# Expert weights in long rows per partition, the hidden rows turned on VectorE, six weight buffers

## What is computed

```python
def expert_choice_ffn(h, w_router, w_gate, w_up, w_down):
    b, s, d = h.shape                       # 1, 256, 1024
    cap = CAPACITY_FACTOR * s // N_EXPERTS  # 32 tokens for each of 16 experts
    aff = jax.nn.softmax((h @ w_router).astype(jnp.float32), axis=-1)
    gates, idx = lax.top_k(jnp.swapaxes(aff, 1, 2), cap)
    xs = jax.vmap(lambda hb, ib: hb[ib])(h, idx)
    hid = jax.nn.silu(jnp.einsum('becd,edf->becf', xs, w_gate)) * jnp.einsum('becd,edf->becf', xs, w_up)
    out = jnp.einsum('becf,efd->becd', hid, w_down) * gates[..., None].astype(h.dtype)
    return jax.vmap(lambda ob, ib: jnp.zeros((s, d), h.dtype).at[ib.reshape(-1)].add(ob.reshape(-1, d)))(out, idx)
```

## Time and profile before

| | |
|---|---|
| median of three runs | 2667.03 us (2659.16 to 2667.18) |
| the profiled execution's own time | 2660.17 us |
| its span, first to last instruction | 2658.4 us |
| TensorE matmul, busy | 2062.7 us, 78% of the span |
| VectorE, busy | 723.2 us, 27% |
| ScalarE, busy | 538.4 us, 20% |
| moved from HBM | 736.88 MB, mean 278 GB/s |

### The profile page before, as it was taken

The page is one execution under the profiler, slowest core; times in us unless marked ns, Lnnn a source line. Parts: engine busy times, 40 slices in busy tenths (PEclk is TensorE's granted clock), DMA queues, the critical chain, the costliest instruction groups (busy, mean ns, idle before and its releaser), DMA issues.

```text
span 2658.4 us, 30415 instructions
## 1 busy us (share of the span) xinstructions
PE 2062.7 (78%) x13332; PEld 1230.3 (46%) x13332; DVE 723.2 (27%) x1115; ACT 538.4 (20%) x816; POOL 105.8 (4%) x145
## 2 busy tenths in 40 slices
PE   8899899989998998896666766666676667666765
PEld 8779798887897886774111111111111112111211
DVE  4554544454545445543000000000000000000001
ACT  5444333343444333332000000000000000000000
POOL 2100100011001001100000000000000000000000
PEclk9879899997998999878665666666666756565566
DMA  8225376742434766327999999999999999999997
GB/s 263 80 88 167 104 237 211 226 136 81 143 128 148 224 221 207 124 110 282 391 381 390 410 381 370 393 392 377 371 408 383 372 366 412 382 367 375 409 385 240
DMA packets 269380, 739.92 MB, mean 278 GB/s; under 512 B 10768, under 2 KB 137232, under 8 KB 236352
## 3 DMA queue, kind: packets, MB, share of 16 engines
q1 hardware_dynamic: 266896, 731.29, 75.9%
q0 software_dynamic: 2352, 6.69, 0.7%
HBM read 736.88 MB, written 1.05 MB: 278 GB/s over the span
## 4 chain that ended last, share of the span: by engine, by line
DMA 47%; PE 40%; DVE 7%; ACT 3%; issue 2%; SPq 1%; POOL 0%; DVEq 0%; ACTq 0%
PE PS L310 39%; DMA WB<-in_w_up 13%; DMA WB<-in_w_gate 12%; DMA WB<-in_w_down 6%; DMA J<-in_w_gate 2%; DMA J<-in_w_up 2%; DMA N<-in_w_up 2%; DMA N<-in_w_gate 2%; DVE WL L1380 2%; ACT WH L917 1%; DMA C<-in_w_gate 1%; DMA C<-in_w_up 1%; SPq L2215 1%; DMA N<-in_w_down 1%; DMA J<-in_w_down 1%
## 5 line engine op out<-in xcount | busy, mean ns | idle before, releaser
L310 PE MATMUL PS<-WB,XS 128*32 128x352 f32 x2880 | 379.5, 672 | 130.3 <-DMA WB<-in_w_up 74.8
L1380 DVE TENSOR_TENSOR WL<-W,WH 128x2048 fp32r<-128x2048 f32 x136 | 313.7, 2307 | 244.0 <-ACT WH L917 244.0
L310 PE MATMUL PS<-WB,S 128*32 128x512 f32 (+1 forms) x1072 | 207.2, 885 | 143.1 <-DMA WB<-in_w_down 141.3
L310 PE MATMUL PS<-HTh,WH 128*128 128x256 f32 x1064 | 307.7, 289 | 5.7 <-DVE HTl L1831 2.6
L917 ACT ACTIVATE WH<-W 128x2048 fp32r<-128x2048 f32 x141 | 269.0, 1908 | 178.7 <-PE PS L310 174.7
L310 PE MATMUL PS<-HTl,WH 128*128 128x256 f32 x1064 | 301.5, 283 | 0.0
L310 PE MATMUL PS<-HTh,WL 128*128 128x256 f32 x1064 | 301.4, 283 | 0.0
L310 PEld LDWEIGHTS PS<-WB,XS 128*32 128x32 f32 x2880 | 98.7, 140 | 403.7 <-DMA WB<-in_w_up 176.3
L1375 DVE SCALAR_TENSOR_TENSOR S<-S,PS 128x352 f32<-128x352 f32 (+1 forms) x110 | 63.3, 588 | 758.5 <-ACT S L1341 719.7
L310 PEld LDWEIGHTS PS<-HTh,WH 128*128 128x128 f32 x1064 | 204.4, 192 | 9.3 <-DVE WL L1380 3.3
L310 PEld LDWEIGHTS PS<-HTl,WH 128*128 128x128 f32 x1064 | 204.6, 192 | 0.3
(11 more groups left out here) (282 smaller groups left out, 2430.4 us busy)
## 6 DMA issues: line engine op xcount, KB each, us to landing
WB<-in_w_gate SPq DMA_DIRECT2D x91, 1408.0 KB, 28.3
WB<-in_w_up SPq DMA_DIRECT2D x89, 1408.0 KB, 30.0
WB<-in_w_down SPq DMA_DIRECT2D x112, 1024.0 KB, 15.9
W<-in_w_in SPq DMA_DIRECT2D x31, 1024.0 KB, 5.6
W<-in_w_ada SPq DMA_DIRECT2D x24, 1024.0 KB, 5.3
W<-in_w_gate SPq DMA_DIRECT2D x22, 1024.0 KB, 7.8
W<-in_w_up SPq DMA_DIRECT2D x22, 1024.0 KB, 5.6
W<-in_w_down SPq DMA_DIRECT2D x22, 1024.0 KB, 5.1
```

What stands on the lines that cost most here:

```text
L310: return e.matmul(o, l, r, start=start, stop=stop, skip_group_check=True)
L1380: e.tensor_tensor(M.WL[i][:, :], M.W[:, 2048 * (m % NW):2048 * (m % NW) + 2048], M.WH[i][:, :].bitcast(F32), ALU.subtract).then_inc(*up("l ...
```

## The change

All 48 expert matrices are read in the same way. A matrix is seen as 128 long rows: partition p gets rows 8p to 8p+7 of w_gate or w_up, or rows 22p to 22p+21 of w_down, 90,112 contiguous bytes in either case. Four chunks cut these in pieces of 22,528 bytes, each one transfer over 128 partitions. There are six buffers of that size, five in a new `WB` and one over constants and work space in `C1`. A buffer now serves two k of gate or up (freed after the second), or 11 half rows of 512 columns of w_down.

As a contraction chunk k of gate and up now holds the rows 8p+k, everything that makes the other operand steps by eight: the turning of the normed x, the gather, the router's load, the norm's gains, and sections 3 and 4 of the ada vector, whose units do eight matmuls with 32 stationary columns and one moving column in place of two with 128.

In w_down a partition p = 32q+c holds rows 704q + 22c + u. Its operand is thus `HD` with every 32 x 32 block (tokens by c) transposed, for each u, which one VectorE transpose does; the seven TensorE transposes, two banks and the copies fall away. Down has 44 matmuls of 512 columns and 128 rows; u modulo 4 picks the group of PSUM partitions. Both scatters follow after the last chunk.

Other tensors are laid out anew: `XS`, `XP`, `SEL` under the old `S`, `HF`, `YA` and `W1` in `N1`, `HD`, `HH`, `SG`, `DN` elsewhere in `S`. At first use the six buffers wait: the first for V, U and G, the second for the last attention use, the third and fourth also for the last units' splits, the fifth and sixth also for the mixer's output.

```diff
--- before.py
+++ after.py
@@ -61,7 +61,7 @@
 
 
 NW = 4
-NB = 7
+BIG = 5632
...
+
+    M.PLACE = [(10240 + BIG * i, 10240 + BIG * i + BIG) for i in range(5)]
+    M.PLACE.insert(1, None)
+    M.BIG = [WB[:, BIG * i:BIG * i + BIG] for i in range(5)]
+    M.BIG.insert(1, C1[:, 320:320 + BIG])
 
     def view(a, *shape):
         v = M.S[:, a:a + math.prod(shape)]
...
@@ -267,14 +272,11 @@
     M.WS, M.LN = view(5888, 8, 128), view(6912, 2, 512)
     M.AT, M.GM = view(7936, 2, 512), view(8960, 2, 512)
 
-    M.SLG = view(1152, 2, 512)
-    M.HD = [view(2176 + 704 * i, 704) for i in range(2)]
-    M.HH = [view(3584 + 896 * i, 7, 128) for i in range(2)]
-    M.DN = [view(5376 + 1024 * i, 2, 512) for i in range(2)]
-    M.SG = [view(7424 + 256 * i, 256) for i in range(2)]
-    M.W1, M.R4 = view(7936, 4, 256), view(8960, 2, 128)
-    slots = [M.WB[:, 2816 * i:2816 * (i + 1)] for i in range(NB)]
-    M.BIG = slots[0:3] + M.MORE[0:2] + slots[3:] + M.MORE[2:]
+    M.HD = [view(4096 + 704 * i, 704) for i in range(2)]
+    M.HH = [view(5504 + 704 * i, 22, 32) for i in range(2)]
+    M.SG = [view(6912 + 256 * i, 256) for i in range(2)]
+    M.R4 = two(M.D3)
+    M.DN = [view(8192 + 1024 * i, 2, 512) for i in range(2)]
...
                 for t in range(2):
                     o, i = ps[:, k, 128 * t:128 * t + 128], srcs[t][:, 128 * (k0 + k):128 * (k0 + k) + 128]
+                    if eighths:
+                        i = srcs[t].rearrange("p (q k) -> p k q", k=8)[:, k0 + k, :]
                     ins = e.transpose(o, i, M.ID) if by is None else mm(o, i, by[:, 128 * t:128 * t + 128], True, True)
...
+        elif n // 4 in (3, 4):
+            j, ad = n % 4, M.AD.rearrange("p (q k) -> p k q", k=8)
+            for k in range(8):
...
             for j in range(2):
-                ins = mm(ps, M.XP[j][:, t, 128 * k:128 * k + 128], M.SEL[:, t, :], t == j == 0, t == j == 1)
+                ins = mm(ps, M.XP[j][:, t, :].rearrange("p (q k) -> p k q", k=8)[:, k, :], M.SEL[:, t, :], t == j == 0, t == j == 1)
         ins.then_inc(*up("full", "xs", k))
...
                 *up("full", "scat", ex, hf, t))
+
+    def down(ex, i):
+
+        v, hh = chunk().rearrange("p (s d) -> p s d", d=512), M.HH[ex % 2]
+        if i == 0:
+            e.wait_ge(*at("turned", ex))
+        halves = range(11 * i, 11 * i + 11)
+        for hf in range(2):
+            if i == 0:
+                if ex:
+                    e.wait_ge(*at(f"dn{hf}", ex - 1))
+                else:
+                    e.wait_ge(C.sig.sem(f"bank{hf}"), C.banks.n[hf])
+            for s in halves:
+                if s % 2 == hf:
+                    u = s // 2
+                    g = 32 * (u % 4)
+                    ins = mm(PS[g:g + 32, 4 + hf, :], hh[:, u, :], v[:, s - 11 * i, :], u < 4, u >= 18)
+            if hf:
+                taken(ins)
+            elif i == 3:
+                ins.then_inc(*up("down4", ex, 0))
+        if i == 3:
...
@@ -840,7 +863,8 @@
             for k in range(8):
                 if ex == m == 0 and k < 6:
                     gather(k + 2)
-                buf = chunk()
+                if k % 2 == 0:
+                    buf = chunk()
                 if ex == m == 0:
                     e.wait_ge(*free("xs", k))
                 if k == 0:
...
+                        c0 = 2816 * (k % 2) + 704 * q + 352 * hf
                         ins = mm(PS[32 * q:32 * q + 32, 2 * m + hf, 0:352], lhs, buf[:, c0:c0 + 352], k == 0, k == 7)
-                taken(ins)
+                if k % 2:
+                    taken(ins)
             same(("gu", ex, m), ("chunk", C.loads - 1))
         turn_gates(ex)
-        turn_hidden(ex)
...
+        for i in range(4):
+            down(ex, i)
+        for hf in range(2):
+            scatter(ex, hf)
...
-            s = {0: 0, 1: 8, 3: 16, 4: 24}[sec] + 2 * j
-            o = K["MT"][:, s:s + 2]
-            e.tensor_tensor(o, ps[:, 256:258], par("b_ada", 8 * sec + 2 * j, 2), ALU.add).then_inc(*freed("ada", n))
+            if sec < 2:
+                s = 8 * sec + 2 * j
+                o, b, i = K["MT"][:, s:s + 2], par("b_ada", s, 2), ps[:, 256:258]
+            else:
+                o, b, i = (v[32 * j:32 * j + 32] for v in (K["MT"][:, 8 * sec - 8:8 * sec], par("b_ada", 8 * sec, 8), ps[:, 256:264]))
+            e.tensor_tensor(o, i, b, ALU.add).then_inc(*freed("ada", n))
...
@@ -1995,13 +1989,10 @@
             e.wait_ge(*at("gate", ex, hf))
             e.wait_ge(*at("gu", ex, 1))
             stt(o, o, 0.5, u, ALU.mult, ALU.mult).then_inc(*up("hidden", ex, hf))
-        ps = full("hid", ex, 1)
-        hh = M.HH[e2]
         if ex >= 2:
             e.wait_ge(*at("hh_free", ex - 2))
-        e.tensor_copy(hh[:, 4, :], ps[:, 0:128])
-        e.tensor_copy(hh[0:64, 5, :], ps[0:64, 128:256])
-        e.tensor_copy(hh[64:128, 5, :], ps[64:128, 256:384]).then_inc(*freed("hid", ex, 1))
+        e.wait_ge(*at("hidden", ex, 1))
+        e.transpose(M.HH[e2][:, :, :], M.HD[e2].rearrange("p (c u) -> p u c", u=22)).then_inc(*up("turned", ex))
...
             e.wait_ge(*at("chunk", c - nbuf))
-        elif i in (3, 4):
+        elif M.PLACE[i] is None:
             e.wait_ge(*C.free("o2", 7))
-            e.wait_ge(*C.free("turn", ("at",), 2))
-        elif i == nbuf - 1:
-            e.wait_ge(*at("x", "mix2", 1, 1))
         else:
-            j = i if i < 3 else i - 2
-            lo, hi = 2816 * j, 2816 * (j + 1)
+            lo, hi = M.PLACE[i]
             e.wait_ge(*at("full", "v", 1, 3))
-            if hi > 4608:
-                e.wait_ge(*at("full", "ug", 1))
+            e.wait_ge(*at("full", "ug", 1))
             for m in range(n - NW, n):
-                if 8704 + 2048 * (m % NW) < hi and 8704 + 2048 * (m % NW + 1) > lo:
+                if 18944 + 2048 * (m % NW) < hi and 18944 + 2048 * (m % NW + 1) > lo:
                     e.wait_ge(*at("low", m))
-            if hi > 16896:
+            if hi > 27136:
                 e.wait_ge(*at("y", "mix2"))
         c += 1
...
     for ex in range(16):
-        for wname in ("w_gate_2", "w_up_2"):
-            for k in range(8):
+        for wname in ("w_gate_2", "w_up_2", "w_down_2"):
+            w = D[wname][0, ex].rearrange("(p r) d -> p (r d)", p=128)
+            for i in range(4):
                 buf, sem, key = buffer()
-                e.dma_start(buf, D[wname][0, ex, 128 * k:128 * k + 128, :]).then_inc(*up(sem, key, by=16))
-        w = D["w_down_2"][0, ex].rearrange("(q j) d -> j q d", q=4)
-        for jt in range(6) if ex < 15 else (5, 0, 1, 2, 3, 4):
-            for nh in range(2 if jt < 5 else 1):
-                buf, sem, key = buffer()
-                if jt < 5:
-                    e.dma_start(buf[:, 0:2048].rearrange("p (q d) -> p q d", q=4),
-                                w[128 * jt:128 * jt + 128, :, 512 * nh:512 * nh + 512]).then_inc(*up(sem, key, by=16))
-                else:
-                    v = buf[:, 0:2048].rearrange("p (q d) -> p q d", q=2)
-                    e.dma_start(v[0:64], w[640:704, 0:2, :]).then_inc(*up(sem, key, 0, by=16))
-                    e.dma_start(v[64:128], w[640:704, 2:4, :]).then_inc(*up(sem, key, by=16))
+                e.dma_start(buf, w[:, BIG * i:BIG * i + BIG]).then_inc(*up(sem, key, by=16))
...
```

More of the change, by code:

```diff
@@ L375, in out_unit, with turning @@
         return y_unit(name, l, n, part(MX, slice(None), slice(2 * n, 2 * n + 2)), y, **kw)
-    def turning(name, srcs, chunks, by=None):
+    def turning(name, srcs, chunks, by=None, eighths=False):
         for k0 in range(0, chunks, 2):
@@ L385, in turning, with norming, pre_norm @@
             yield
-    def norming(name, src=X, dg=M.DG):
+    def norming(name, src=X, dg=M.DG, eighths=False):
         yield
         e.wait_ge(*at("diag", name))
-        yield from turning(name, [src[:, 0, :], src[:, 1, :]], 8, dg)
-    def pre_norm(name):
-        for _ in norming(name):
+        yield from turning(name, [src[:, 0, :], src[:, 1, :]], 8, dg, eighths)
+    def pre_norm(name, eighths=False):
+        for _ in norming(name, eighths=eighths):
             pass
@@ L815, in turn_gates @@
         ins.then_inc(*up("full", "sg", ex))
-    def turn_hidden(ex):
-        hd = M.HD[ex % 2]
-        e.wait_ge(*at("hidden", ex, 1))
-        for g, grp in enumerate(((0, 1, 2, 3), (4, 5, 6))):
-            ps = spare(("hid", ex, g))
-            for n, j in enumerate(grp):
-                s0, wd = (0, 128, 256, 384, 512, 640, 576)[j], 64 if j == 5 else 128
-                ins = e.transpose(ps[0:wd, 128 * n:128 * n + 128], hd[:, s0:s0 + wd], M.ID)
-            ins.then_inc(*up("full", "hid", ex, g))
     def scatter(ex, hf):
@@ L833, in scatter @@
                 *up("full", "scat", ex, hf, t))
+    def down(ex, i):
[19 more added lines that the diff above has]
+        if i == 3:
+            same(("down4", ex, 1), ("chunk", C.loads - 1))
     for ex in range(16):
@@ L1337, in scalar_program @@
         if ex >= 2:
-            e.wait_ge(*at("full", "hid", ex - 2, 1))
```

(6 more changed lines are left out.)

83 lines of the change are left out of this document (24 added, 59 removed).

## The result

The changed kernel takes 2527.69 us (median of 4 runs, 2525.98 to 2528.66), the kernel before 2665.55 beside it (2659.16 to 2667.18). The ratio is 0.9486, with a 95% interval of 0.9469 to 0.9504. The forecast was 2525.0 in 2498 to 2575. The profiled execution after has 2525.98 us, its span is 2524.2 (before: 2658.4).

What follows compares the result with a forecast made beforehand. The prediction took DMA delivery in the 16-expert loop as the bound. Loop and first refill -142.5, front +4 and tail +3 gave -135.5 us against 2660.17, so 2525 us, range 2498 to 2575.

Steps and rivals of the forecast that it cites:

- front: Ahead of the expert loop: 3 us for the ada units and 1 us for strided weight reads, +4 us.
- tail: From last chunk's landing to closing norm: 13.0 to 14.5 us where it was 10.7, taken as +3 us.
- The pairs' term: Expert loop, last w_down chunk sent as two 64-partition transfers: 8.75 us falls to 2.47, 100.5 us less over 16.
- The chunk's term: Expert loop: each 2,883,584-byte chunk takes 6.78 us, the pace of 11,264-byte rows; 186 chunks make 1261.1 us.
- The ada units: Ahead of the loop: eight one-column matmuls instead of two in eight units cost 3 us of 0 to 8.
- The step of eight elements: Ahead of the loop: transposes and gather matmuls reading weights with that step cost 1 us, between 0 and 7.
- the buffers and the turning: Expert loop: fewer, larger buffers cost nothing; one VectorE transpose, about 1 us, lies under 27 us of queued loads.
- rival 1: Loop loads: 22,528-byte rows are cut up; at 410 GB/s a chunk takes 7.03 us, +47, 2572 us; chance 0.06.
- rival 2: Loop loads: spacing in HBM costs, everything runs at 387 GB/s, 7.45 us a chunk, +125, 2650 us; chance 0.03.
- rival 3: Loop loads: engines meet in the same memory part; 8.24 us a chunk, +271, 2796 us, slower; chance 0.05.
- rival 4: Expert loop: TensorE binds if w_down's column groups do not overlap; the stage grows by 660 us; chance 0.01.
- rival 5: Expert loop: DMA dips have another cause than the half-partition pairs and stay, +37, 2562 us; chance 0.09.

Runs made afterwards that it cites:

- experiment 1: Kernel before with the two 64-partition transfers of each expert's last w_down chunk replaced by one over 128 partitions: 2575.82 us, ratio 0.9667.
- experiment 2: Kernel before with every w_down chunk loaded as 128 contiguous pieces of 8,192 bytes: 2537.64 us, ratio 0.9524.
- experiment 8: Changed kernel with five weight buffers instead of six: 2534.51 us, ratio 0.9486, loop 1265.9 us.
- experiment 4: Changed kernel with each chunk as two transfers over 128 partitions with pieces of 11,264 bytes: 2543.70 us, ratio 0.9546.
- experiment 11: Changed kernel with the eight ada units back to two matmuls with 128 weight columns: 2522.52 us in one run.
- experiment 6: Changed kernel with the last w_down chunk of every expert as two transfers of 64 partitions: 2785.81 us, ratio 1.0403.
- experiment 12: Changed kernel plus four full-size matmuls per head in the attention of the first block's second layer: 2529.41 us, ratio 0.9481.
- experiment 9: Changed kernel with three weight buffers instead of six: 2548.39 us in one run, loop 1279.4 us.
- experiment 10: Changed kernel with the VectorE transpose of the hidden rows done four times instead of once: 2524.19 us, ratio 0.9460.
- experiment 3: Changed kernel with each chunk read from one contiguous 2.9 MB in HBM: median 2518.17 us, ratio 0.9451, loop 1259.7 us.
- experiment 5: Changed kernel with each chunk as two transfers of 2,816-byte pieces: 2623.26 us, ratio 0.9821, loop 1364.8 us.

## Why the prediction was right, and where its numbers were off

The forecast of -135.5 us met -134.2 on the span. In parts it reads: loop -144.9 (measured -151.9), first refill +2.4 and front +4, so +6.4 (measured +16.0), tail +3 (measured +1.6). (The forecast took 2638.94 for the last landing before; with that boundary the loop measures -149.2 and the tail -1.0.) The total is better than its parts: loop and tail came out 8.4 us better than forecast and the front 9.6 us worse. That these cancel to little over 1 us is luck.

**The mechanism was right.** The loop is what the DMA engines deliver, and both losses named in it were there, shown apart by experiments 1 and 2. The loop's gain of 151.9 us divides into 91.0 for the pairs, 36.1 for the 2,048-byte pieces, and 24.8 for the step from the second experiment's kernel to the changed one. Of these 24.8, some 6.7 are one more chunk's worth in the prefetch, by experiment 8, and the other 18 the step from 11,264 and 8,192 bytes to 22,528; experiment 4, which goes back to 11,264, gives 16.0 of them.

**The pairs' term was too large.** I had 8.75 us a pair, 6.28 of them to be gained against a chunk of 2.47; by the runs a pair took 8.4, 5.9 to be gained, which makes 6 us less for all sixteen. Two things are in it. I took 2638.94 for the landing of the last chunk. It is the last but one; the last lands at 2641.5 while TensorE is in the scatter, and the trace of before has its matmuls behind that, without a wait for a transfer:

```profile
2645.01 1.07 PE L310 MATMUL PS<-WB,S 128*32 128x512 f32 x8
```

Then the rest to be shared by 16 pairs would have been 142.7 us. But not all of it is theirs: by the same terms the loop of experiment 1 comes to 2.3 + 833.9 + 176 x 2.70 = 1311.4 us and measures 1320.0. That kernel has no pairs, so these 8.6 us aren't theirs: 1.7 fall in the first expert, and the rest comes in single longer intervals all along the loop (an expert takes 84.4 us in the mean, where the terms give 83.9). So 134.1 / 16 = 8.4 a pair, 5.7 above a chunk of 2.70, which is what experiment 1 took away. The doubt that I kept, 37 us, was for the larger part unfounded: the slow slices of one view at 1400 to 1500 were too few to price a dip that was longer elsewhere.

**The chunk's term was a little too dear.** Most chunks land 6.71 us apart in place of 6.78, which gives 13 us: I kept the nearest row, and a longer row did run a little faster. But 186 x 6.71 = 1248.1, and 1259.1 measured leaves 11.0 where I had 2.3 of latency. The first chunk is 8.9 us from issue to landing (2.2 of the 11.0), the second comes 8.1 behind it (1.4), and the other 7.4 are single intervals of up to 7.8 us, spread over the whole loop (the landings at 1419, 1649, 1885, 2115 and 2351 us are the longest). In the mean a chunk comes every 6.76 us. What makes the long intervals stays open. Net the loop came out 4.3 us shorter than the forecast's 1263.4.

**The front was the part that failed.** I allowed 4 us and got 13.6. Some 9 of them stand in the two places where the change altered instructions, and the forecast's terms for both were too small.

The ada units were to cost 3 us (0 to 8) and cost 4.9, at a granted clock of 1.00 before and after; experiment 11 gives 4.2 of them back. In the kernels that keep the new units they cost 4.9 to 5.8.

The step of eight elements was to cost 1 us. I named the 16 transposes of the normed x and priced only the gathers. The transposes take 7.9 us where they took 5.6, and the logits behind them 5.4 where they took 3.7. Windows of before, both in the transposes:

```profile
1204.20:1207.20 3.00, 3.00 (x15) 3.00 (x15) 2.95 (x4) 0.40 (x1) 0.00 (x0) 0.50 0.99 420
1207.70:1209.20 1.50, 1.50 (x15) 1.50 (x15) 0.54 (x2) 1.02 (x2) 0.00 (x0) 1.00 1.01 410
```

and of after:

```profile
1214.00:1217.00 3.00, 3.00 (x15) 3.00 (x14) 2.71 (x4) 0.10 (x1) 0.00 (x0) 0.50 1.06 452
1217.40:1220.90 3.50, 3.50 (x16) 3.50 (x16) 0.99 (x2) 1.02 (x2) 0.00 (x0) 1.00 0.96 377
```

At half clock both do 15 records in 3.00 us. At full clock the old form does 15 in 1.50 us and the strided one 16 in 3.50: it gains nothing from the clock. The logits' own instructions are the same as before; 3.6 us of them now run at a granted clock of 0.50, where all ran at 1.00. Together this stage costs 4.0 us, and set beside before it costs 3.9 to 4.2 in ten of the eleven profiled executions with the new layout (5.6 in the other) and nothing in the two of experiments 1 and 2, which keep the old. No run takes out the step alone. For the gathers the forecast held: their weight loads went from 227 ns to 331, but the three that stand ahead of the first expert took 4.58 us in all against 4.64 before, and the five inside it 1.36 each against 1.20.

The rest, some 4.5 us, is the same instructions at another clock. Windows of before:

```profile
113.00:126.00 13.00, 13.00 (x46) 8.31 (x45) 5.15 (x24) 4.53 (x15) 0.00 (x0) 0.63 0.00 1
```

and of after:

```profile
113.00:126.00 13.00, 13.00 (x40) 8.29 (x39) 4.68 (x19) 4.57 (x14) 0.00 (x0) 0.50 0.01 1
```

In this attention, which the change doesn't touch, TensorE's granted clock fell to half earlier in the profiled execution after, and it left 3.3 us later. A second attention, near 1136 to 1150 us of before, added 2.9, and 1.4 were won back at 1071 to 1074, where before ran at half clock. That the change brings these on is not shown, and two things speak against it: the kernel of experiment 1, with the old layout, lost 4.8 us itself in the first attention (105 to 134 us), and those of experiments 6 and 12 lost nothing in the second attention. The first refill comes at 1242.4 to 1253.3 in the kernels with the new layout (at 1227.3 in one, see the last part) and at 1230.3 to 1235.5 in those with the old; the 9 us are most of that.

**Prefetch and tail.** The six chunks were in at 1231.6 and not at 1218.5, since the issues at 1191.3 moved with the front to 1200.8 and the last two came at 1207.3; they were still ahead of the first expert, so nothing hung on it. The tail is 9.7 us from the last landing to the closing norm, 8.1 before. I had 13.0 to 14.5, with the down matmuls at half clock. The last chunk ran at a granted clock of 1.00 and took 3.62 us.

**Nothing for the buffers and the turning** was right, and had more room than I gave it (experiments 8 to 10). I counted on four queued chunks of cover; even two beyond the one in use do.

**The rivals.** 1 falls by the packets of 22,528 bytes. 2 and 3 fall by experiment 3. The Trainium skill, "DMA: Bandwidth & Descriptors", section "Latency and other measured facts", warns of row pitches of 512 KiB and more; by the run a pitch of 88 KiB costs nothing, and larger ones no run here shows. 4 falls by the idle time of TensorE and 3.62 us a chunk. 5 falls by experiment 1.

## What to carry to other kernels

Where a loop is bound by its loads, read the GB/s in steps of a few microseconds and not the busy share: engines that showed a busy share of 1.0 delivered 216, 387, 424 or 430 GB/s. Take out transfers over half the partitions first; then make the pieces long, with most of the gain reached at 8 KB. Count buffers by the wait they must cover: here the fourth to sixth earned only their share of the prefetch. And where a new order of the weights makes the other operand strided, price every instruction that reads it with the step, at full clock.

## What the runs showed of the hardware that I had not expected

**Half the partitions, half the pace, and more when repeated.** A transfer over 64 partitions ran at some 216 GB/s, half of the 433 beside it. The Trainium skill, "SBUF — State Buffer", section "Door 1: The DMA port swizzle", says that the pace of a transfer depends on how many of 16 ports its partitions reach, and by its formula partitions 0 to 63 reach eight. The 216 agree. Why a pair costs 9.5 us alone and 17.7 as one of sixteen no run here explains.

**More than the share of HBM.** One core alone was delivered 430 GB/s throughout. The Trainium skill, "DMA: Bandwidth & Descriptors", section "Where 436 GB/s comes from", puts the limit from HBM at about 358 GB/s for a core; the loop contradicts that, here with one core at work, and stays just under the 435 that the same section gives for the fabric.

**Weights read with a step of eight elements gain nothing from the full clock.** The transposes of the normed x took 0.20 us a record at half clock with and without the step, and at full clock 0.22 with it and 0.10 without (windows above).

**A stretch that runs at half clock in one execution and at full clock in the next.** From 640 to 680 us, in the first block's second attention, TensorE runs without idle time in one execution as in the other. Window 640 to 650 of the changed kernel:

```profile
640.00:650.00 10.00, 10.00 (x32) 6.50 (x31) 2.59 (x13) 1.74 (x6) 0.00 (x0) 0.50 0.00 0
```

and of the kernel with 2,816-byte pieces, whose front is the same:

```profile
640.00:650.00 10.00, 10.00 (x56) 6.81 (x55) 4.81 (x25) 4.35 (x16) 0.00 (x0) 1.00 0.00 1
```

A head takes 6.36 us in the first and 3.55 in the second, and the first refill comes about 20 us earlier (1227.3). The four runs of experiments 3 and 5 fall in two groups just 20 us apart, and so I compared loops and not totals there. What decides it stays open. More matmuls of full size in that stage (experiment 12) didn't. A kernel whose runs spread by 20 us ahead of the part that is being studied hides an effect of that size in the totals.
